# A hybrid decoder layer on one core: weights asked for between the row stores, four finished rows scaled by VectorE in the next group, the mixer's loads in turning order, w_o through four rooms

## What is computed

```python
def mixer(h, ...):
    p = h @ w_in                                  # 24 tiles of 128 columns, and 8 more columns
    qkv, new_buf = causal_conv(p[..., :QKV_DIM], conv_buf, conv_w)
    q, k, v = heads of silu(qkv), q and k l2-normed
    o, S = gated_delta_chunked(q, k, v, gdec, beta, S0)      # needs the inverse of (1 + strict lower part) per chunk
    o_a = rmsnorm(o, o_norm_g) * silu(gate)
    o_b = spatial_gate(u, rmsnorm(p[..., OFF_V:], v_norm_g), w_s, b_s)
    return concatenate([o_a, o_b]) @ w_o

def ffn(h, w_up, w_down):
    return square(relu(h @ w_up)) @ w_down        # 1024 -> 4096 -> 1024

x = x + mixer(rmsnorm(x));  x = x + ffn(rmsnorm(x));  y = rmsnorm(x, norm_f_g)
```

## Time and profile before

| | |
|---|---|
| median of 3 runs | 2656.99 us (2654.3 to 2657.12) |
| the profiled execution | 2655.33 us |
| its span (first to last instruction) | 2653.2 us |
| mean granted TensorE clock | 0.97 |
| TensorE busy | 2480.3 us, 93% of the span |
| VectorE, ScalarE, GpSimd busy | 1412.9, 700.0, 251.5 us |
| moved by DMA | 210.12 MB, mean 79 GB/s |

### The profile page before, as it was taken

How to read it: one execution, slowest core, us unless ns; L and a number is a source line. 1 busy time by engine, 2 the same in 40 slices (tenths; PEclk the granted TensorE clock), 3 DMA queues, 4 the chain that set the end, 5 groups by cost and what they waited for, 6 DMA issues and landing times.

```text
span 2653.2 us, 36483 instructions
## 1 busy us (share of the span) xinstructions
PE 2480.3 (93%) x13808; PEld 2256.9 (85%) x13808; DVE 1412.9 (53%) x2445; ACT 700.0 (26%) x1425; POOL 251.5 (9%) x421
## 2 busy tenths in 40 slices
PE   5999999995699998579999999999799999999997
PEld 4899999995588886379999999998689898998986
DVE  4545555674566664565454545454754554545455
ACT  4323332211444443032121212122312122121212
POOL 3100011000333330110000000000400000000002
PEclk9999999997799999789999999999899999999999
DMA  4123344313444542141111111111412111111201
GB/s 138 49 72 102 105 123 121 115 64 140 136 141 142 147 147 76 32 175 48 48 47 47 47 47 47 47 48 56 151 32 64 32 47 47 47 47 32 63 24 72
DMA packets 213336, 210.12 MB, mean 79 GB/s; under 512 B 30315, under 2 KB 184107, under 8 KB 209898
## 3 DMA queue, kind: packets, MB, share of 16 engines
q1 hardware_dynamic: 213234, 208.73, 25.3%
HBM read 159.00 MB, written 49.79 MB: 79 GB/s over the span
## 4 chain that ended last, share of the span: by engine, by line
PE 53%; DVE 1%; DMA 1%; POOL 1%; issue 1%; ACT 0%; SPq 0%; DVEq 0%; ACTq 0%; POOLq 0%
PE bank L122 17%; PE bank L124 17%; PE bank L123 17%; PE bank L1905 1%; PE bank L1903 1%; PE bank L1949 0%; DMA out_y_prompt_dram<-f_acc 0%; DVE f_h_lo L1827 0%; DMA f_dn_raw<-in_w_down_dram 0%; DMA f_up_raw<-in_w_up_dram 0%; DVE f_acc L1772 0%; DVE f_acc L152 0%; DVE f_z L1794 0%; DVE f_xn L1816 0%; DVE f_dn_lo L1780 0%
## 5 line engine op out<-in xcount | busy, mean ns | idle before, releaser
L1772 DVE TENSOR_TENSOR f_acc<-bank,f_acc 128x512 f32<-128x512 f32 x512 | 351.3, 690 | 298.8 <-PE bank L124 298.8
L122 PE MATMUL bank<-f_h_hi,f_up_lo 128*128 128x344 f32 (+1 forms) x1536 | 491.7, 320 | 4.0 <-DVE f_h_lo L1827 2.9
L124 PE MATMUL bank<-f_h_hi,f_up_hi 128*128 128x344 f32 (+1 forms) x1536 | 490.3, 319 | 0.0
L123 PE MATMUL bank<-f_h_lo,f_up_hi 128*128 128x344 f32 (+1 forms) x1536 | 490.1, 319 | 0.0
L122 PE MATMUL bank<-f_dn_hi,f_z 128*128 128x512 f32 x1024 | 400.0, 391 | 1.1 <-DVE f_acc L1772 1.1
L123 PE MATMUL bank<-f_dn_lo,f_z 128*128 128x512 f32 x1024 | 399.5, 390 | 0.0
L124 PE MATMUL bank<-f_dn_hi,f_z 128*128 128x512 f32 x1024 | 399.5, 390 | 0.0
L122 PE MATMUL bank<-h_hi,w_lo 128*128 128x412 f32 (+3 forms) x1000 | 351.1, 351 | 1.6 <-issue 1.6
L123 PE MATMUL bank<-h_lo,w_hi 128*128 128x412 f32 (+3 forms) x1000 | 349.9, 350 | 0.0
L124 PE MATMUL bank<-h_hi,w_hi 128*128 128x412 f32 (+3 forms) x1000 | 349.8, 350 | 0.0
L1787 DVE TENSOR_TENSOR f_sqr<-f_relu 128x344 f32<-128x344 f32 (+1 forms) x192 | 100.7, 525 | 365.0 <-ACT f_relu L1709 363.6
(11 more groups left out here) (358 smaller groups left out, 2968.9 us busy)
## 6 DMA issues: line engine op xcount, KB each, us to landing
f_up_raw<-in_w_up_dram SPq DMA_DIRECT2D x64, 512.0 KB, 4.7
f_dn_raw<-in_w_down_dram SPq DMA_DIRECT2D x64, 512.0 KB, 3.3
p_dram<-y SPq DMA_DIRECT2D x24, 1024.0 KB, 4.6
w_raw<-in_w_in_dram SPq DMA_DIRECT2D x24, 512.0 KB, 5.5
xres<-in_x_prompt_dram SPq DMA_DIRECT2D x16, 512.0 KB, 4.5
x_dram<-x SPq DMA_DIRECT2D x16, 512.0 KB, 3.0
f_acc<-x_dram SPq DMA_DIRECT2D x16, 512.0 KB, 8.1
out_y_prompt_dram<-f_acc SPq DMA_DIRECT2D x16, 512.0 KB, 2.7
```

Source lines behind the costliest of these rows:

```text
L122: pe.matmul(out, wl, xh, start=start and k == 0, stop=False, skip_group_check=skip)
L123: pe.matmul(out, wh, xl, start=False, stop=False, skip_group_check=skip)
L124: last = pe.matmul(out, wh, xh, start=False, stop=stop and k == n - 1, skip_group_check=skip)
L1772: dve.tensor_tensor(dst, bank, dst, ALU.add).then_inc(s["y_added"], 1)
```

## The change

Three places change.

1. **project**: the inverses are stored in two parts: rows 0 to 47 in tile t = 23, once step j = 46 is done, and rows 48 to 63 after the last tile. The memset of the diagonal goes from the last step to the first.
2. **mix**: w_o comes through four rooms, in the order 4 to 7, 0 to 3, and tiles 4 to 7 of that order are asked for after pass 0's share of SP. Part 0 of the first output product waits for four cuts, part 1 for eight. The residual rows of chunk 0 now wait for six cuts. For chunk 0 alone the inputs are asked for in the order in which TensorE turns them. The gains come ahead of w_s; masking, turning and copying w_s go behind pass 0 on their engines, and so does ScalarE's `decay` behind its two copies in pass 0. Three semaphores are doubled, one for each room.
3. **ffn**: SP asks for `up` 2 right behind the in-place loads, then stores rows 0 to 3 with no loads between them, then asks for `down` 1, `up` 3, the four rows, `down` 2, and stores rows 4 to 7. VectorE scales rows 4 and 5 after tile 0 of group 0 of the second block, rows 6 and 7 after tile 1; GpSimd's eight products go. There are four semaphores for stores instead of two, so a store of the second block waits for the landing of the one four back.

The diff, cut to its core:

```diff
+EARLY_ROWS = 48
-    def store_blocks(self, sp):
-        sp.wait_ge(self.s["tb_made"], 1)
-        sp.dma_start(self.io["t_dram"], self.blk.rearrange("p i j -> p (i j)")).then_inc(self.s["tb_stored"], 16)
-        sp.wait_ge(self.s["tb_stored"], 16)
+    def store_blocks(self, sp, part):
+        rows = (slice(0, EARLY_ROWS), slice(EARLY_ROWS, HALF))[part]
+        sp.wait_ge(self.s["tb_made"], 1 + part)
+        sp.dma_start(self.io["t_dram"].rearrange("p (i j) -> p i j", j=HALF)[:, rows, :], self.blk[:, rows, :]).then_inc(self.s["tb_stored"], 16)
...
         if j == 1:
             dve.wait_ge(s["blk_loaded"], 16)
+            dve.memset(self.blk.rearrange("p i j -> p (i j)")[:, 0:HALF * HALF:HALF + 1], 1.0)
...
-        if j == HALF - 2:
-            dve.memset(self.blk.rearrange("p i j -> p (i j)")[:, 0:HALF * HALF:HALF + 1], 1.0).then_inc(s["tb_made"], 1)
+        if j in (EARLY_ROWS - 2, HALF - 2):
+            dve.sem_inc(s["tb_made"], 1)
...
-            keys.store_blocks(eng)
+                if t == NT - 2:
+                    keys.store_blocks(eng, 0)
+            keys.store_blocks(eng, 1)
+            eng.wait_ge(keys.s["tb_stored"], 32)
...
+WO_ROOMS = 4
+WO_ORDER = [*range(H, KT), *range(H)]
-    wo_raw = (x1[1][:], xres[1][:])
+    wo_raw = (x1[0][:], xres[0][:], x1[1][:], xres[1][:])
...
-        if (o, half, part) == (0, 0, 0):
-            pe.wait_ge(wo_lo_made, KT)
+        if o == 0 and half == 0:
+            pe.wait_ge(wo_lo_made, (H, KT)[part])
...
-        if F:
-            act.wait_ge(s["gb_loaded"], 16 * (f + 1))
...
+        if F and f > 0:
+            decay(act, f)
...
             act.activation(gt[:], bE, ACT.Copy).then_inc(s["g_copied"], 1)
+        if f == 0:
+            decay(act, f)
...
+        for part in ((values, queries, keys_tile, gmlp_rows, decay, inverse) if f == 0 else
+                     (inverse, queries, decay, keys_tile, values, gmlp_rows)):
+            part()
...
-        wait(sp, wo_lo_made, k - 1)
-        sp.dma_start(wo_raw[k % 2], io["w_o"][0, k * P:(k + 1) * P, :]).then_inc(wo_loaded[k % 2], 16)
+        wait(sp, wo_lo_made, k - WO_ROOMS + 1)
+        at = WO_ORDER[k] * P
+        sp.dma_start(wo_raw[k % WO_ROOMS], io["w_o"][0, at:at + P, :]).then_inc(wo_loaded[k % WO_ROOMS], 16)
...
-            if r == 1:
-                sp.wait_ge(wo_lo_made, KT)
+            if r < 2:
+                sp.wait_ge(wo_lo_made, KT - 2 + 2 * r)
             wait(sp, s["x1_made"], 2 * (r - 1))
             sp.dma_start(xres[r % 2][:], io["x_prompt"][0, rows_of(r), :]).then_inc(s[f"xres_loaded{r % 2}"], 16)
...
-        if n < 2:
-            for k in (range(2, 6) if n == 0 else range(6, KT)):
-                load_w_o(sp, k)
...
-            load_w_o(sp, 0)
-            load_w_o(sp, 1)
+            for k in range(WO_ROOMS):
+                load_w_o(sp, k)
             for n in range(PASSES + 1):
                 sp_pass(sp, n)
+                if n == 0:
+                    for k in range(WO_ROOMS, KT):
+                        load_w_o(sp, k)
...
-            w_pe(pe)
-            pe.wait_ge(ws_copied, 1)
             for n in range(PASSES):
                 pe_pass(pe, n)
+                if n == 0:
+                    w_pe(pe)
+                    pe.wait_ge(ws_copied, 1)
...
-                if blk == 1:
-                    for p in range(2):
-                        weights(NTL + p, p, p + 2, p + 1)
-                    for m in range(IN_PLACE, NBT):
-                        eng.wait_ge(stored[m % 2], 16 * (m // 2))
-                        store_rows(0, m)
...
                     for m in range(IN_PLACE, NBT):
                         load_in_place(m)
-                    for m in range(IN_PLACE + 2):
-                        if m >= 2:
-                            eng.wait_ge(stored[m % 2], 16 * (m // 2))
-                            load_rows(1, m + 2)
-                        if m < IN_PLACE:
-                            store_rows(0, m)
+                    up_weights(NTL, 0, 2)
+                    for m in range(IN_PLACE):
+                        store_rows(0, m)
+                    down_weights(NTL, 1)
+                    up_weights(NTL + 1, 1, 3)
+                    for m in range(IN_PLACE, NBT):
+                        eng.wait_ge(stored[m % IN_PLACE], 16)
+                        load_rows(1, m)
+                    down_weights(NTL + 1, 2)
+                    for m in range(IN_PLACE, NBT):
+                        store_rows(0, m)
...
-            pool.wait_ge(out_made[0], IN_PLACE)
-            for m in range(IN_PLACE, NBT):
-                row = slot(0, m)
-                pool.tensor_tensor(row, row, finals[0].rs[:, m:m + 1].to_broadcast([P, D]), ALU.mult).then_inc(row_scaled, 1)
-                pool.wait_ge(row_scaled, m - IN_PLACE + 1)
-                pool.tensor_tensor(row, row, fgain[:], ALU.mult).then_inc(out_made[0], 1)
...
+                    if between:
+                        between(j)
...
+            def rest(j):
+                for m in range(IN_PLACE + 2 * j, IN_PLACE + 2 * j + 2):
+                    finish(0, m)
+            group(1, 0, 0, False, rest)
+            group(1, 1, 1, False)
+            with dve.Fori(1, NG // 2 - 1) as ii:
```

120 lines of the change are left out of this document (70 added, 50 removed).

## The result

| kernel | median us (runs) | profiled execution / its span |
|---|---|---|
| before | 2656.35 (4 runs, 2654.3 to 2657.12) | 2655.33 / 2653.2 |
| changed | 2620.09 (4 runs, 2619.52 to 2620.75) | 2619.52 / 2617.8 |

The ratio is 0.9865, 95% interval 0.9848 to 0.9882: the changed kernel is 1.35% faster. Between the two profiled executions lie 35.8 us.

What follows compares the result with a forecast made beforehand. TensorE, busy 93% of the span, was taken as the bound, so gains come where it idles: 3.7 + 15.0 + 15.6 = 34.3 off 2655.3 gives 2621; with 1.7 for the median 2622.7, stated as 2622.5, range 2610 to 2635.

Steps and rivals of the forecast that it cites:

- The hole: Mixer, pass 2: TensorE stands still for 6 to 7 us, after two output products, until the values land.
- its gate: Mixer, pass 2: SP's wait for six w_o cuts before the first residual rows holds all nine tiles; opens at M+43.1.
- Projection's end: End of projection: with 1.5 MB of inverses stored earlier, the last store lands 3.7 us earlier; bounds 2.5 and 4.9.
- Start of pass 1: Mixer, M being its start: values at M+23.5, R's product at M+25.5, 12.1 us earlier; bounds M+22 to M+30.
- The four cuts no longer wait for a second trip: Mixer entry: four w_o tiles requested at once spare the cuts a second trip; part of the 12.1 us.
- I cost both at nothing; without the cover they'd cost some 2 us: Mixer, pass 0: moving w_s's constants and the activation table load under TensorE's wait costs nothing; uncovered, some 2 us.
- The up to 2 us for large tiles ahead of the small inverse rows: Mixer entry: large tiles going ahead of small inverse rows in the queue are worth up to 2 us.
- Pass 2: Mixer: pass 2 and everything after it come 15.0 us earlier; bounds 9 and 25.
- The loss in the slow clock: Mixer, pass 2: half clock after the hole and a gate tile 0.2 late take 2.8 us off 17.8.
- Between the blocks: Between the MLP's two token blocks: 16.9 less 1.3 gives 15.6 us gained; bounds 10 and 16.9.
- the change takes away all three: MLP gap: late weights request, w_down tile taking 7.94 us, and VectorE's cut at 3.36 us beside GpSimd all go.
- no hole in pass 2: Rival, mixer: the residual's gate opens earlier or tiles land within 3 us; gain up to 25, 2612.5 us; chance 12%.

Runs made afterwards that it cites:

- run 6: The changed kernel with two rooms for w_o instead of four, requested where the kernel before did; half of w_o first stays: 2619.76 us, ratio 0.9865.
- runs 4 and 5: run 4, and the changed kernel with w_s's constants and ScalarE's exponentials ahead of pass 0 and pass 0's tiles in old order: 2630.14 us, ratio 0.99.
- run 4: The changed kernel with mask, turn and copy of w_s ahead of pass 0 again, every DMA as changed: 2630.48 us, ratio 0.9902.
- Run 8: The changed kernel with first residual rows requested behind all pass 2 tiles, and of those values, gate and gMLP rows first: 2613.70 us, ratio 0.9844.
- run 10: The changed kernel with the next two MLP tiles' weights requested behind the stores and loads of rows again: 2622.84 us, ratio 0.9875.
- run 12: The changed kernel with SP's whole old queue between the MLP's blocks, VectorE still scaling rows 4 to 7: 2627.89 us, ratio 0.9893.

## Why the prediction was right, and where its steps were not

The time was forecast as 2622.5 and is 2620.09, inside the range. The hole, its gate and the gap of the MLP came as described; the start of pass 1 came at the right time for another cause than the one named, which is luck. By its steps:

- **Projection's end**, 3.7 forecast, 3.8 in the trace, 4.0 in the run by itself. The small store landed 4.8 us after its request, at 637.6. Right, with the spread of the mixer's start said above: the means of the traces with and without the early store lie 3.0 apart.
- **Start of pass 1**: values at M+23.5 forecast, turned at M'+23.1; R's product at M+25.5 forecast, at M'+26.6. The times were right, and the cause was not. "The four cuts no longer wait for a second trip" is worth nothing by itself (run 6). The turning order is worth nothing with the constants in front (runs 4 and 5) and is untested with them behind. The step that failed is "I cost both at nothing; without the cover they'd cost some 2 us": with the constants ahead of pass 0 the kernel is 10.4 us slower and its mixer 9.3 us longer (run 4). The sum took R as ready soon after w_o's tiles have landed, at about M+22, and never followed pass 0 on TensorE and VectorE, behind which the cuts stand. R is made from M'+22.6 on (661.33) only because the constants had moved; with them in front it is made 32.3 us after the mixer's start (672.20 in run 4). I looked at R's wait of 8.55 us, which names w_o's cuts, but not at what had delayed pass 0 before them. The old entry's 7.85 us of matmuls in 25 said it: TensorE's first turn waited 15.6 us into the mixer for a mask. The up to 2 us for large tiles ahead of the small inverse rows stands in no run.
- **Pass 2**: the start at M+36 (M'+35.8 measured), the gate at M+43.1 (M'+42.0), the values at M+52.8 (M'+52.4), the tile landing after 5.5 where the row has 5.0. The hole was 9.39 us and not 6 to 7: I had counted the output products to M+46, and they end at 681.7, M'+43.0. The hole's length doesn't enter the sum, its end does. Run 8 shows the mechanism, at 6.4 us. The Trainium skill ("DMA: Bandwidth & Descriptors", the section on the anatomy of one DMA) has a fit, for another issuing path, that gives an estimate of 2.6 us for a transfer of this size. As the first request of the changed mixer (638.71) such a tile landed in 2.7 us, as by the fit; here, behind eight others asked for in the 4.8 us before it, it took 5.5, so the row was the better source.
- **The loss in the slow clock** was set at 2.8 with the late gate tile, and this term was too large. The values of pass 2 are turned 18.2 us earlier than before, counted from the mixer's start (17.8 forecast), and R's product comes 16.5 earlier, so 1.7 are lost. The gate tile caused no wait, and R's product already took the 1.06 us of the full clock; only the turns and one product ran at half. 18.2 - 1.7 against 17.8 - 2.8 is the mixer's 16.5 against 15.0.
- **Between the blocks**: 15.6 forecast, 15.0 by the marker; TensorE's waits 0.6 and 0.7 forecast, 1.0 and 0.5 in the trace. The step "the change takes away all three" was right in that queue and GpSimd's rows both count (leaving the queue old costs 8.1, leaving the rows old 1.9, both together 15.0), but its first cause, the late request, was given too much: my expectation of run 10, 6 to 9 us of standing for asking behind stores that don't wait, was wrong (3.3 us in its trace). Asking later costs 2.7 by the marker, the landings between the requests bring it to 8.1 (run 12).
- **Rivals**: none of them happened. The chance of 12% for "no hole in pass 2" rested on a gate that might open early; it needed the edit of run 8.

## What to carry to other kernels

When a wait names its last releaser, follow the stage in front of it too: here the wait for w_o's cuts hid 9 to 10 us that the mask of another constant had cost one pass earlier. In a queue that is issued in order, put requests whose room is free ahead of any that wait for a landing or for another engine's last step, and test a "more buffers" edit by itself, since it may only move the wait. Where two edits cure the same gap, undo each alone and both: here their prices didn't add (6.9 and 13.1 or 1.9 and 8.1).

## What the runs showed of the hardware

- In these rows VectorE beside GpSimd on tiles in SBUF is not slowed evenly, it is held. In the run with GpSimd's rows a 128x344 product that takes 0.52 took 2.02, from 1878.44 to 1880.46, while GpSimd's row product ran from 1877.85 to 1880.09. A 128x344 square took 1.63 and a 128x8 product 1.67; they end at 1883.11 and 1884.88, and GpSimd's products at 1882.74 and 1884.87. Each time VectorE's operation ends with GpSimd's or within 0.4 us of it. The square that VectorE began at 1877.82, just ahead of GpSimd's product, took its usual 0.52, and that GpSimd product 2.24 where the one at 1887.50 took 1.89. The Trainium skill ("SBUF — State Buffer", the section on its two separate sides) says that the two share a port pair as an exclusive lock for a whole instruction; the trace agrees.
- The granted clock averaged 0.64 over the hole of pass 2 (681.68 to 691.07, no matmul) and was 0.50, the level of 1.2 GHz, from 685.00 on. It averaged 0.59 over the 4.23 us of matmuls behind the hole, and was 1.00 from 695.30 on. In run 12 it averaged 0.62 over the last 5 us of a wait of 7.4 us (1885 to 1890) and was 0.50 for 1890 to 1895, while matmuls ran again. In the changed kernel's MLP, where the waits are 1.0 and 0.5 us, it was 1.00 from 1863 to 1910.
- The time from SP's request to the landing depended on what had been asked for just before. A tile of 256 KB took 2.7 us as the changed mixer's first request, 5.5 us behind eight others in pass 2, and 8.4 us in run 8, where it was asked for at 664.02 behind four tiles of w_o of 512 KB each.
